# Expert steps of an MoE layer: one 128-row block in three f32r products, or two 64-row parts in plain f32 with weights in two fixed places

## The reference

```python
scores = sigmoid(u @ router_w)                  # 512 tokens, 128 experts
_, idx = top_k(scores + router_b, 8)            # 8 experts for each token: 4096 pairs
wts = s_sel / sum(s_sel) * 2.5
# every pair (token, expert e), grouped by expert:
g, up = split(u_row @ w_gu[e], 2)               # w_gu[e] 1024 x 512, f32, 2 MB
y = (silu(g) * up) @ w_down[e]                  # w_down[e] 256 x 1024, f32, 1 MB
out[token] += wts * y
```

## Time and profile before

| | |
|---|---|
| median of 3 runs | 1383.23 us (1381.11 to 1386.07) |
| the profiled execution, first to last instruction | 1379.5 us; no other time is given for it |
| PE, weight loads, DVE, ACT, POOL busy | 97%, 72%, 61%, 47%, 14% |
| PE time of the expert loop | busy in all of 603 to 1315 us |

### The profile page before, as it was taken

The page is one execution under the profiler, slowest core; times in us unless marked ns, Lnnn a source line. Parts: engine busy times, 40 slices in busy tenths (PEclk is TensorE's granted clock), DMA queues, the critical chain, the costliest instruction groups (busy, mean ns, idle before and its releaser), DMA issues.

```text
span 1379.5 us, 26382 instructions
## 1 busy us (share of the span) xinstructions
PE 1334.8 (97%) x5922; PEld 988.0 (72%) x5923; DVE 842.4 (61%) x1367; ACT 644.7 (47%) x817; POOL 196.5 (14%) x328
## 2 busy tenths in 40 slices
PE   5899999999999999899999999999999999999985
PEld 5778877778888788567777777677777776776732
DVE  4432574865535877777664767766676655465427
ACT  4571246455132313356664656655665544454311
POOL 1000000000000000322222222222222222222200
PEclk9899999999999999999999999999999999999998
DMA  9432111332736852669986869979797866586276
GB/s 328 139 121 61 62 61 62 122 122 79 243 102 229 263 165 89 230 231 314 338 283 220 312 231 344 360 273 349 270 353 272 293 229 237 206 278 216 81 295 275
DMA packets 104719, 301.33 MB, mean 218 GB/s; under 512 B 20540, under 2 KB 23844, under 8 KB 95720
## 3 DMA queue, kind: packets, MB, share of 16 engines
q1 hardware_dynamic: 78808, 258.20, 53.8%
q0 software_dynamic: 20800, 33.61, 7.0%
q10 hardware_dynamic: 5072, 9.02, 1.9%
HBM read 319.61 MB, written 40.90 MB: 261 GB/s over the span
## 4 chain that ended last, share of the span: by engine, by line
PE 93%; DVE 3%; ACT 2%; issue 1%; DMA 1%; DVEq 0%; SPq 0%; ACTq 0%
PE psum L1549 30%; PE psum L1770 28%; PE psum L1811 17%; PE psum L1757 5%; PE psum L1522 2%; PE psum L1802 2%; PE psum L1835 1%; PE psum L1696 1%; PE psum L1826 1%; PE psum L1651 1%; PE psum L1582 1%; DMA ring<-in_ada_w 1%; PE psum L1640 1%; PE psum L1611 1%; PE psum L1706 1%
## 5 line engine op out<-in xcount | busy, mean ns | idle before, releaser
L1413 DVE TENSOR_TENSOR gu_lo<-gu_raw,gu_hi 128x1024 f32 x204 | 241.6, 1222 | 93.1 <-ACT gu_hi L946 79.5
L946 ACT ACTIVATE gu_hi<-gu_raw 128x1024 f32 x204 | 211.5, 1056 | 113.7 <-issue 63.5
L1811 PE MATMUL psum<-w_dn,mask 128*128 x560 | 251.6, 592 | 0.0
L1811 PEld LDWEIGHTS psum<-w_dn,mask 128*128 128x128 f32 x560 | 105.9, 189 | 106.1 <-issue 100.6
L1770 PE MATMUL psum<-gu_hi,xT_hi 128*128 (+1 forms) x568 | 148.4, 403 | 0.0
L446 DVE TENSOR_TENSOR w_lo<-ring,w_hi 128x1024 fp32r<-128x1024 f32 x80 | 94.9, 1222 | 87.1 <-ACT w_hi L439 85.1
L1770 PE MATMUL psum<-gu_hi,xT_lo 128*128 (+1 forms) x568 | 141.0, 390 | 0.0
L1549 PE MATMUL psum<-uT_hi,w_hi 128*128 128x512 f32 x352 | 139.3, 396 | 1.1 <-DVE w_lo L446 1.1
L1770 PE MATMUL psum<-gu_lo,xT_hi 128*128 (+1 forms) x568 | 140.3, 389 | 0.0
L439 ACT ACTIVATE w_hi<-ring 128x1024 fp32r<-128x1024 f32 x80 | 82.8, 1056 | 121.0 <-PE psum L1549 61.0
L1549 PE MATMUL psum<-uT_hi,w_lo 128*128 128x512 f32 x352 | 137.1, 389 | 0.0
(11 more groups left out here) (302 smaller groups left out, 1927.4 us busy)
## 6 DMA issues: line engine op xcount, KB each, us to landing
gu_raw<-in_exp_w_gu SPq DMA_DIRECT2D x208, 512.0 KB
w_dn<-in_exp_w_down SPq DMA_DIRECT2D x70, 1024.0 KB
ring<-in_w_in SPq DMA_DIRECT2D x56, 512.0 KB, 5.3
ring<-in_ada_w SPq DMA_DIRECT2D x32, 512.0 KB, 5.0
ring<-expert_rows SPq DMA_DIRECT2D x8, 1024.0 KB, 12.2
ring<-in_ada_w SPq DMA_DIRECT2D x4, 1024.0 KB, 13.2
scale_w<-in_ada_w SPq DMA_DIRECT2D x4, 1024.0 KB, 14.6
ring<-in_w_branch_b SPq DMA_DIRECT2D x8, 512.0 KB, 6.0
```

Source lines behind the costliest of these rows:

```text
L946: act.activation(gu_of(gu_hi, order, p), gu_raw[:, PK * p:PK * p + PK], ACT.Copy).then_inc(gu_hi_ready, 1)
L1413: tt(gu_of(gu_lo, order, p), gu_raw[:, PK * p:PK * p + PK], gu_of(gu_hi, order, p).bitcast(F32), ALU.subtract).then_inc(gu_split, 1)
L1811: mm = pe.matmul(moe_bank(Y0 + g), hT[:, j], w_dn[:, bass.ds(order % 3, 1), j, g * NC:(g + 1) * NC].rearrange("p o n -> p (o n)"), start=( ...
```

## The change

A step now takes two parts of 64 rows, each with an expert of its own. The 98 parts are cut into two streams of 49, and step n takes part n of stream 0 and part n of stream 1. Matmuls of stream 0 use TensorE's cell columns 0 to 63, those of stream 1 columns 64 to 127. All are plain f32 on the weights as loaded, so the splitting on ACT and DVE is gone, and `gate_up` has 16 matmuls instead of 24, the down product 8 instead of 4. The weights of a stream have one place, `w_now[:, q]`: 2 MB of gate and up, loaded in two halves of 1 MB once `gate_up` of the step before has used that half (`gu_used`), and 1 MB of down, loaded once the step before is through its down product (`y_psum`). A load is skipped on the chip (`cond`) where the stream's expert stays. A tile `held` of 72 KB in each partition is declared and not used in the loop. Before the loop, the plan's tables are made for two streams, and the shared expert's gate and up weights go to `ring`; behind it, `final_g` and the shared down weights are loaded once the loop's loads are done.

```diff
+STREAMS = 2
+W = P // STREAMS
+PARTS = (T * TOP_K - E) // W + E
+MOE_BLOCKS = -(-PARTS // STREAMS)
...
+        held = sb("held", [P, 3, 6, D], F32, moe)
+        w_now = sb("w_now", [P, STREAMS, 6, D], F32, moe)
+        gu_part = lambda q, k: w_now[:, q, k // 2, (k % 2) * NC:(k % 2 + 1) * NC]
+        dn_part = lambda q, j, g: w_now[:, q, 4 + j, g * NC:(g + 1) * NC]
...
+            def load(n):
+
+                turns = [sp.value_load(step_load[0:1, bass.ds(STREAMS * n + q, 1)], min_val=0, max_val=TABLE) for q in range(STREAMS)]
+                chosen = [sp.value_load(step_expert[0:1, bass.ds(STREAMS * n + q, 1)], min_val=0, max_val=E - 1) for q in range(STREAMS)]
+                for g in range(2):
+
+                    sp.wait_ge(gu_used, 2 * n - 1 + g)
+                    for q in range(STREAMS):
+                        sp.dma_start(w_now[:, q, 2 * g:2 * g + 2].rearrange("p a n -> p (a n)"), gu_half(chosen[q], g),
+                                     cond=turns[q] > 0, bounds_check="skip_entire_dma").then_inc(gu_in[q][g], 16)
+                sp.wait_ge(y_psum, n + 3)
+                for q in range(STREAMS):
+                    sp.dma_start(w_now[:, q, 4:6].rearrange("p a n -> p (a n)"), dn_whole(chosen[q]),
+                                 cond=turns[q] > 0, bounds_check="skip_entire_dma").then_inc(dn_in[q], 16)
+
+            for i, s, b in live_blocks(sp):
+                load(b + 1)
...
+            def gate_up(n, s):
+
+                pe.wait_ge(xT_ready, n + 1)
+                for g in range(2):
+                    for q in range(STREAMS):
+                        pe.wait_ge(gu_in[q][g], 16 * n + 16)
+                    for k in range(4 * g, 4 * g + 4):
+                        for q in range(STREAMS):
+                            at = slice(q * W, q * W + W)
+                            mm = pe.matmul(moe_bank(GU)[at, :], xT[:, s % 2, k, at], gu_part(q, k), start=(k == 0), stop=(k == KT - 1))
+                    mm.then_inc(gu_used, 1)
...
             for i, s, b in live_blocks(pe):
-                order = pe.value_load(order_of[0:1, bass.ds(b, 1)], min_val=0, max_val=E)
-                after = pe.value_load(order_of[0:1, bass.ds(b + 1, 1)], min_val=0, max_val=E)
-
                 turn_rows(b + 2, (s + 2) % UNROLL, 16 * (i + (s + 2) // UNROLL) + 16)
-                find(b + AHEAD)
                 pe.wait_ge(h_ready, b + 1)
                 for j in range(2):
                     mm = pe.transpose(moe_bank(HT)[:, j * P:(j + 1) * P], h_tok[:, bass.ds(j, P, 2)], ident[:])
                 mm.then_inc(hT_psum, 1)
-                gate_up(b + 1, s + 1, after)
+                find(b + AHEAD)
+                gate_up(b + 1, s + 1)
 
                 pe.wait_ge(hT_ready, b + 1)
-                pe.wait_ge(w_loaded[s], 16 * i + 16)
+                for q in range(STREAMS):
+                    pe.wait_ge(dn_in[q], 16 * b + 16)
                 pe.wait_ge(y_ready, b + 2)
                 for g in range(2):
                     for j in range(2):
-                        mm = pe.matmul(moe_bank(Y0 + g), hT[:, j], w_dn[:, bass.ds(order % 3, 1), j, g * NC:(g + 1) * NC].rearrange("p o n -> p (o n)"),
-                                       start=(j == 0), stop=(j == 1))
+                        for q in range(STREAMS):
+                            at = slice(q * W, q * W + W)
+                            mm = pe.matmul(moe_bank(Y0 + g)[at, :], hT[:, j, at], dn_part(q, j, g), start=(j == 0), stop=(j == 1))
                 mm.then_inc(y_psum, 1)
```

More of the change, by code:

```diff
@@ L46 @@
 AHEAD = 4
+STEPS = SPANS * SPAN * UNROLL + 2 * UNROLL
 BANK_STEPS = 5, 7, 1, 2
@@ L261, in layer_program @@
         hT = mask[:, 0:2]
[L263 to L267, removed]
+        live_row = rows[0:1, 0:TABLE]
+        expert_row = rows[0:1, 256:256 + TABLE]
+        fresh_row = rows[0:1, 512:512 + TABLE]
+        turn_row = rows[0:1, 768:768 + TABLE]
+        by_step = lambda row, q: row[:, 0:TABLE].rearrange("o (n q) -> o q n", q=STREAMS)[:, q]
+        sgate = tmp_tok[:, 0].rearrange("p (j n) -> p j n", j=2)
         moe.close()
@@ L336, in layer_program @@
         xT_ready = sem("xT_ready")
[L337 to L343, removed]
+        gu_in = [[sem(f"gu_in{q}_{g}") for g in range(2)] for q in range(STREAMS)]
+        dn_in = [sem(f"dn_in{q}") for q in range(STREAMS)]
+        gu_used = sem("gu_used")
         silu_done = sem("silu_done")
@@ L458, in slots_of @@
         def slots_of(t):
-            return (slots_a, slots_b, slots_c)[t % 3]
-        def gu_of(w, order, p):
-            return w[:, bass.ds(order % 2, 1), PK * p:PK * p + PK].rearrange("p o k f -> p (o k) f")
+            return slots[:, t % 3]
         x_rows = x[0].rearrange("(t p) d -> p t d", p=P)
@@ L529, in _, with dn_whole @@
+            def dn_whole(e):
+                return expert_dn[bass.ds(e, 1)].rearrange("o p j n -> p (o j n)")
             sp.wait_ge(first_ready, 1)
[L530 to L533, removed]
-            sp.wait_ge(tables_ready, 1)
[L536 to L562, removed]
-            live_n = sp.value_load(live_count[0:1, 0:1], min_val=1, max_val=MOE_BLOCKS)
[L564 to L569, removed]
+            experts = []
@@ new lines, in _ @@
+            for i, s, b in live_blocks(sp):
+                load(b + 1)
+            live_n = sp.value_load(live_count[0:1, 0:1], min_val=1, max_val=MOE_BLOCKS)
+            sp.wait_ge(xT_psum, live_n + 2)
+            landed = sp.snap(live_n * 16 + 16)
+            for q in range(STREAMS):
+                sp.wait_ge(dn_in[q], landed)
+            for s in range(UNROLL):
+                sp.wait_ge(gathered[s], (live_n + AHEAD - 1 - s) // UNROLL * 16 + 16)
+            sp.dma_start(row_a[:], final_g.rearrange("(o d) -> o d", o=1).broadcast_to([P, D])).then_inc(fg_in, 16)
@@ L1747, in find @@
                 for t in range(TT):
-                    mm = pe.matmul(moe_bank(IDX)[:, 0:6], pick[:, t], pick_cols[:, t], start=(t == 0), stop=(t == TT - 1))
+                    for q in range(STREAMS):
+                        at = slice(q * W, q * W + W)
+                        mm = pe.matmul(moe_bank(IDX)[at, 0:6], pick[:, t, at], pick_cols[:, t, q], start=(t == 0), stop=(t == TT - 1))
                 mm.then_inc(idx_psum, 1)
@@ L1789, in _ @@
             find(3)
-            gate_up(0, 0, 0)
+            gate_up(0, 0)
             wait_emptied(pe, ("sgu", 1))
```

214 lines of the change are left out of this document (72 added, 142 removed).

## The result

The changed kernel takes 1841.44 us (median of 4 runs, 1835.38 to 1846.5) against 1383.36 (4 runs): 1.331 times the time before, 95% interval 1.3266 to 1.3355. The profiled execution is one of 1836.85 us with a span of 1835.1, so 84 us more than the 1751 of the sum. I read the page first: slices and queues as in the earlier trace rows, then the costliest groups as in the earlier trace rows.

The account below looks back on a forecast made before the run. PE was taken to bound the expert loop, 716 us of the run. Loop +364, gate_up(0) +1.4, before the loop +3, tail +3: 1379.5 + 371 = 1751 us span, about 1755 us median, range 1650 to 1920.

Parts of the forecast that it names:

- the 1751 of the sum: Whole kernel: forecast span in us, the earlier span of 1379.5 plus 371, of which the loop is +364.
- take turns: Rival, PE's products: column halves do not overlap, 1.72 us a pair instead of 0.86; about 2255 us, chance 0.11.
- open weight loads: Rival, PE's products: halves overlap but 48 weight loads a step are not hidden, 4.5 us; about 1975 us, chance 0.06.
- Issue: 3.6: SP in the loop: first gate and up load issued 3.6 us after the down product's end.
- a = 2 keeps the queues busy: Loop loads: two fresh experts' down weights in step n make the first gate and up half land 2 us later.
- a = 1: Step class: a counts fresh experts in step n, whose down weights load first; a = 1 was given no added delay.
- c = 1: Step class: c counts fresh experts in step n+1; c = 1 forecast at 22.1 us, 24.1 with a = 2.
- The table's last column: Forecast whole-step times by a and c, 17.3 to 26.5 us; the last but one column holds measured times.
- Skipped loads: 6: Loop steps with c = 0: skipped transfers taken as counted up 6 us after the down product's end.
- Clock: 2.0, or 1.0 for c = 0: Start of gate_up: PE at 1.2 GHz after idling costs 2.0 us a step, 1.0 where c = 0.
- The tail: +3: Behind the loop: late final_g and shared down weights, 3.6 transfer and 2.5 fixed, where PE idled 4.5 anyway: +3 us.
- loads in time: Rival, the loop: loads land in time, 49 x 11.9 = 583 us, kernel 1257 us; chance 0.03.

Follow-up runs that it names:

- e1: Changed kernel with gate and up loads of step b+2 asked for before the wait for step b's down product: 1338.54 us, 0.9684 of the time before.
- e7: Changed kernel with stream 1's matmuls, all but the last of each product, on columns 0 to 63 like stream 0's: 2228.56 us.
- e9: Changed kernel with both load groups still behind the down product's wait, but gate and up weights issued first, down weights after: 1621.37 us.
- e10: e1 plus final_g and the shared down weights loaded before the loop, into space freed from held: 1326.72 us, 0.9601 of the time before.
- e2: Changed kernel with the streams' matmuls not alternating: four of stream 0 then four of stream 1 per gate_up half, down product likewise: 1939.54 us.
- e4: Changed kernel with the second gate and up half asked for only when the first half of both streams has landed: 1881.64 us.
- e3: Changed kernel with five unneeded full-width f32 matmuls ahead of each gate_up of the loop, to keep PE busy: 1824.49 us.
- e6: Changed kernel with weights loaded one to three steps ahead into held, then copied by ACT and DVE to w_now: 1349.91 us, 0.9777 of before.

## Why the prediction was right, and where it was off

**The mechanism held.** PE's wait ahead of `gate_up` is there 49 times, ended by transfers into `w_now`, 1.6 to 14.3 us long (4 to 11 were forecast), and it is there because the issue stands behind the wait for `y_psum`: with that order alone changed (e1), 429 of 464 us of it are gone, and 16 us come back ahead of the down product. The 84 us between the sum's 1751 and the measured span are 71 in the loop, 11 in the tail and 2 ahead of the loop.

**PE's step: right.** Pairs cost 0.86 us, and a step with nothing in the way 11.9 (e1). The changes of cell layout cost 0.1 us each, at two places in a step and not three: in e1 the first transposing matmul starts 0.52 us behind the last down record, where 0.43 was due, and the first `find` matmul 0.21 behind the last transposing one, where 0.12 was due. That is some 9 us in all, which the sum had left out and the range allowed. That the halves overlap, taken from row halves, is shown by e7. The rivals "take turns" and "open weight loads" are out. The records of weight loads are hidden too: PE's pitch is 0.43 for each record with the loads of 137 to 168 ns beside it, though both streams use the same rows of cells. So the rule that spoke against the change (the Trainium skill, TensorE: Matmul & The Clock Gate, "The mechanism": a load overlaps only where the row group differs, or by the background buffer) would allow this only by its buffer; no run here tells what hides the loads, only that they are hidden.

**Issue: 3.6, mis-sized.** In steps that load gate and up weights, SP needs 3.9 to 4.0 us where the down weights are skipped and 4.4 to 4.6 where they are loaded. A skipped issue is shorter, 0.1 us instead of some 0.35.

**Landing: the main error.** The prediction's step "a = 2 keeps the queues busy", with nothing for a = 1, was wrong. One fresh expert's down weights, asked for about 4 us earlier, delay the first half by 1.8 us (7.6 against 5.8), two by 2.4. e9 shows that it is they. Together with the later issue this is +2.4 us in 12 steps of c = 1 and +2.6 in 7 of c = 2. With no down weights ahead the first MB takes 5.2 to 5.8 us from the first issue to the start of `gate_up`, and a second 3.1 to 3.6 more (changed kernel with a = 0, and e9), where the sum took 2.5 from the earlier trace rows. Gathers cost 0.3 to 1.1 where gathers and scatters had been given 1.0. The table's last column against its last but one sums to +69 us, step 0 has 2.6 more.

**Skipped loads: 6, measured 5.3.** They count up 0.6 us after the first issue, where I had allowed 2.4. The issue, 1.1 us later than forecast, made up for most of it; that was luck.

**Clock: 2.0, or 1.0 for c = 0.** The 2.0 was right, the 1.0 was not. `gate_up` is 9.0 us long with c = 0 as with c = 1, so it loses 2.0 against e1's 7.06 behind a wait of 5.3 us as behind one of 12. Over the 48 steps that is 95 us, where the prediction had 86. From page to page it is only 87, because e1's own `gate_up` is below full clock in some steps with c = 2.

**The tail: +3, measured +13.7.** I had counted a transfer of 6.1 us behind an idle time of 4.5. But the issue isn't at the loop's end: SP issues `final_g` at 1767.58 and the shared weights at 1767.96, 10 us behind the last down product. Most of the 10 us are the empty rest of the loop: the loop is written for more steps than the 49 live ones, and from 1758.8 to 1765.8 SP tests and branches over 15 that aren't live (L466 to L475). A table read and the arithmetic of the waits take the next 2 us. e10 takes both, transfer and late issue, away and gains 11.8 us over e1.

**What was not asked by the prediction:** how far the change was from a gain. Its rival "loads in time", 1257 us with 49 x 11.9, is not reached even by e1, since the 13 steps in which two experts are fresh are bound by transfers. In e1 they take 60 us more in all than at 11.9 each.

## What to carry to other kernels

Read a queue of loads as a chain: a load waits for every wait that stands ahead of it in its queue, even for another place. When a change takes places away, look first at which waits then come last, and put the load whose place is free first ahead of them. Two half-width streams in two column halves multiply by two experts' weights in the time of one, so a step can need twice the bytes while it gets no longer. Count bytes for each step, and not only on the mean.

## What the runs showed of the hardware

- Column halves in plain f32 overlap wholly (0.43 us for each record of each stream), and beyond program order: matmuls for a free half start while earlier ones for the other half are still waiting to start (e2).
- A skipped 1 MB transfer counts up within 0.6 us of the first issue.
- Transfers asked for some 4 us earlier in the same queue delay a 1 MB transfer by 1.8 to 2.4 us, though the DMA engines have a share of only 0.45 over the loop. A transfer asked for together with it, behind it, does not (e4).
- The ten c = 0 steps of the changed kernel have 3.2 to 4.7 us of idling ahead of `gate_up`, and the granted clock of its first 2 us is 0.51 on the mean, as behind idling of 14 us. In e3, 6.8 us of idling behind 4.6 us of full work were followed by 4 us at 0.50 as well. In e6 even 2.2 us of idling stood ahead of a down product at 0.53 in one step, and ahead of one at 1.00 in another.
